# One triangular inverse corrected once a level and turned for its other form, a recurrence split by directions, and grouped attention heads written by channels

## The chip, the cores and the metric

One core of a Trainium2 chip runs the whole program in one launch. The metric is the device time of that core in microseconds (us). The kernel before took 3077.0 us, the median of three runs (3072.32 to 3078.3).

## The reference, cut to what matters

Two transformer blocks in float32, 512 latent and 256 context tokens, width 1024. The first block mixes tokens with two recurrences (a gated one, HG, and a gated delta rule, DN), then applies a mixture of experts. The second block has attention (four differential heads, eight grouped-query heads of 64 channels sharing two key/value heads), a gated MLP, a spatial gating unit and a second MLP. The adaptive modulation vectors of both blocks are products of a silu vector with a 1024 x 6144 matrix each (three matrices, 24 MB each).

The delta rule needs, for every chunk, direction and head, the solution of a unit lower triangular system, and then a scan over chunks:

```
a_mat = strict_lower(beta * k k^T * decay) + I
u, w  = solve(a_mat, [beta * v, beta * exp(cum) * k])
v_new = u_c - w_c @ state
o     = q_dec @ state + qk @ v_new
state = g_tot * state + k_dec^T @ v_new
```

This kernel takes chunks of 128 tokens (6 of them, `NC`), 4 heads in two passes of 2 (`p` = 0 and 1) and 2 directions, so that a chunk has four 128 x 128 systems. The grouped heads of attention are

```
s = q k^T * 64**-0.5 ; p = softmax(s) ; o = p v      (4 query heads share one k, v)
```

## The kernel before, in words

Each engine has its own instruction stream, and semaphores order them. The program is a list of stages (norm, hg0, hg1, dn0, dn1, wout, moe, proj, attn, awout, ffn0, sgu, ffn1) with a meeting of all engines after each. The change touches dn0 and dn1 (the delta rule's two passes), attn, and awout.

**The modulation chunks.** The product with the modulation matrices is cut into 72 chunks of 1 MB (`pe_mod_chunk`, L378, matmul at L385: four column tiles of 32 columns, each with 512 moving columns). SyncE loads them through a ring of slots, of which four serve these stages; the load of a slot is issued when TensorE has reported its last use. Eight chunks make a group; a group ends with a copy on ScalarE (L418), column sums on TensorE (L396) and a second copy on ScalarE (L424). `pe_mods(pe, W, count, end)` runs `count` chunks at a place of the TensorE program, and `act_mods` runs ScalarE's part at the place that answers to it. The lists at L995 say how many chunks stand where: `DN_MODS[p]` is (first, one per chunk of the system phase, one per unit of the inverse, a pair per step of the recurrence). Before, pass 0 has 8 at the start, none in system and inverse, 2+2+2+2 in the recurrence; pass 1 has 12 in the system phase, 8 in the inverse, 20 in the recurrence.

**Start of dn0** (`pe_dn_first`, L1036; `act_dn_first`, L1267). TensorE projects six tiles of pass 1 (L694, L686), runs 8 chunks (L385), turns the convolved q, k, v (L1048), projects two more tiles (L694) and turns the normed q, k (L1056). VectorE convolves (L1383) meanwhile; its last tap is followed by L1430. ScalarE, in order: the copies of the tiles, its part of the 8 chunks, silu of the convolved tiles (L1273, L1274), then the rest.

**System phase** (6 chunks). TensorE multiplies k k^T (and k q^T) (L1110, L1112) and the decay sums (L1115); GpSimd makes the masks (L1318) and multiplies by beta and the triangle (L1357, L1360, `mask_beta`); ScalarE takes exponentials (L1243); VectorE multiplies (L1455, L1457). In pass 0 the last six tiles of projection stand between the chunks.

**Inverse** (`products` L1138, `corrections` L1148). It is built level by level (7 levels, blocks of 1, 2, ... 64) and kept in two forms, XI and its transpose XT. A unit `u` is one chunk at one level, 42 per pass. GpSimd masks the level out of the system (`al`, L1334, two instructions). Level 0 is transposes (L1133) and subtractions. In each of the 30 units of levels 1 to 5 TensorE makes four products M = al^T XI (L1145), ScalarE copies M (L1252), TensorE makes eight corrections, four for each form (L1155, L1156), and VectorE subtracts them (L1473, L1474). The six units of the last level correct one form only. VectorE also runs two steps of the next pass's convolution per unit in pass 0 (L1383 and its neighbours).

**Recurrence** (6 steps). A step is KS = K dS (L1175), z on VectorE (L1488), U = X z (L1186), times beta on VectorE (L1497), ADD = kx^T dU (L1200), dS on VectorE (L1511). Each of these covers two directions and two heads: four matmuls, then one semaphore. Between KS and U and between U and ADD stand chunks (L385) or, in pass 0, groups of four transposes for pass 1 (`pe_tok_group`, L1077). `norm_steps` for pass 1 is handed out between VectorE's parts from step 3 on, and what is left runs after the last step. Then outputs (L1210, L1211), and in pass 0 more transposes (L1092).

**Attention** (`pe_attn`, L2454; 32 units, `u` from 16 on are grouped heads). TensorE runs scores(u+1) (L2462, eight records of 64 rows), values(u-1) and turn(u) (transposes of the probabilities, L2478). VectorE takes the maxima (L2534), ScalarE two exponentials of 128 x 768 (L2514), VectorE the reciprocals (L2557), and both copy the turned probabilities (L2523, L2525, L2554). scores(u+2) waits for both exponentials of unit u+1. For grouped heads turn(u) waits for the exponentials only; values is 12 matmuls with the turned probabilities as the weights and 64 value columns moving (L2494); VectorE divides by the sum on the way out (L2546). awout then turns all 1024 channels (eight transposes per 128 tokens, L1607), ScalarE copying four (L1648) and VectorE four (L1653), and multiplies by w_out (L1617).

A float32 matmul of 128 x 128 x 128 has two records on TensorE in this trace; a transpose has one.

## Time and profile before

| what | value |
|---|---|
| median of three runs | 3077.0 us |
| the profiled execution | 3088.53 us |
| its span, first to last instruction | 3086.6 us |
| mean granted TensorE clock | 0.956 |
| TensorE busy | 2854.6 us, 92% |
| VectorE, ScalarE, GpSimd busy | 1205.1, 579.2, 432.9 us |
| mean DMA rate | 131 GB/s |

Times below are microseconds from the start of the span. "x8" counts instruction records. A bracket at the end of a timeline row gives the idle time of that engine before the row, and what ended it. The granted clock is a share of full speed (2.4 GHz).

### The profile page before, as it was taken

What the parts mean: (1) busy time and instruction counts of PE and PEld (TensorE: products, weight loads), DVE (VectorE), ACT (ScalarE), POOL (GpSimd) and SP (SyncE); (2) the same over time, 40 slices, a digit from 0 to 9 for tenths busy, and PEclk for the clock granted to TensorE, in tenths of its full rate; (3) what the DMA queues carried; (4) which work ended last, traced back from release to release, by engine and by line L of the source; (5) the groups of instructions that cost most, each with busy time, mean ns of one, the idle gap of its engine ahead of it and who ended that gap; (6) DMA issues with size and microseconds to landing.
All of it is one profiled execution on the core that took longest, in us unless ns stands there. A gap on an engine that the chain in (4) does not pass through costs nothing.

```text
span 3086.6 us, 36191 instructions
## 1 busy us (share of the span) xinstructions
PE 2854.6 (92%) x14765; PEld 2144.3 (69%) x14765; DVE 1205.1 (39%) x2187; ACT 579.2 (19%) x1109; POOL 432.9 (14%) x507
## 2 busy tenths in 40 slices
PE   6999978987978599999999989899999999999998
PEld 4677646975944378788878758578874486688843
DVE  2173642873425211111132485366750102576601
ACT  2102012121201211111132255122110111211200
POOL 2152403525411100000000000000110000000100
PEclk8999978998989699999999999899999999999999
DMA  9211340024271599899982200032222221322220
GB/s 368 75 41 42 110 176 27 3 110 164 83 286 43 192 339 333 322 333 331 323 286 83 69 1 1 1 98 93 82 76 75 92 68 41 99 86 82 89 75 27
DMA packets 202849, 403.15 MB, mean 131 GB/s; under 512 B 12850, under 2 KB 100450, under 8 KB 193506
## 3 DMA queue, kind: packets, MB, share of 16 engines
...
q8 instruction: 91, 1.49, 0.2%
...
## 4 chain that ended last, share of the span: by engine, by line
PE 84%; DVE 6%; DMA 3%; ACT 3%; issue 2%; POOL 1%; ACTq 0%; SPq 0%; POOLq 0%; DVEq 0%
PE ps L2704 17%; PE ps L1891 11%; PE ps L694 7%; PE ps L1909 5%; PE ps L1617 5%; PE ps L2718 5%; PE ps L2320 4%; PE ps L2733 4%; PE ps L2891 4%; PE ps L686 3%; PE ps L764 2%; PE ps L2462 2%; PE ps L385 2%; PE ps L2494 2%; DMA ring<-in_w_mod 2%
## 5 line engine op out<-in xcount | busy, mean ns | idle before, releaser
L1891 PEld LDWEIGHTS ps<-arena,ring 128*128 128x128 f32 x2944 | 334.2, 193 | 13.3 <-issue 10.5
L1891 PE MATMUL ps<-arena,ring 128*128 128x128 f32 x2944 | 334.5, 276 | 2.4 <-DMA ring<-in_w_gate 2.4
L2704 PE MATMUL ps<-arena 128*128 128x256 f32 x1056 | 235.3, 379 | 1.6 <-DVE arena L2801 1.6
L2704 PEld LDWEIGHTS ps<-arena 128*128 128x128 f32 x1056 | 200.5, 190 | 29.6 <-DVE arena L2801 2.4
L1617 PE MATMUL ps<-ring,hT 128*128 128x512 f32 x384 | 172.7, 606 | 4.2 <-DVE arena L2947 2.6
L694 PE MATMUL ps<-hT,ring 128*128 128x512 f32 x384 | 171.5, 601 | 2.5 <-ACT bet L1034 1.8
L2704 PE MATMUL ps<-hT,ring 128*128 128x256 f32 x704 | 164.9, 389 | 3.3 <-ACTq L200 3.3
L1909 PE MATMUL ps<-ring,arena 128*128 128x512 f32 x368 | 164.0, 598 | 1.8
L2704 PEld LDWEIGHTS ps<-hT,ring 128*128 128x128 f32 x704 | 137.5, 196 | 23.8 <-ACTq L200 4.1
L2718 PE MATMUL ps<-ring,arena 128*128 128x512 f32 x352 | 151.5, 592 | 1.3 <-issue 1.3
L2733 PE MATMUL ps<-ring,arena 128*128 128x512 f32 x352 | 151.7, 592 | 0.0
L1334 POOL TENSOR_TENSOR arena<-arena,levm 128x256 f32<-128x256 f32 x168 | 124.4, 764 | 96.3 <-PE ps L1145 87.5
L1617 PEld LDWEIGHTS ps<-ring,hT 128*128 128x128 f32 x384 | 73.3, 195 | 91.3 <-issue 88.9
L2180 DVE TENSOR_TENSOR arena<-arena,ps 128x512 f32<-128x512 f32 x23 | 15.8, 688 | 303.7 <-PE ps L1891 303.7
L694 PEld LDWEIGHTS ps<-hT,ring 128*128 128x128 f32 x384 | 73.0, 193 | 87.0 <-issue 83.1
L2850 POOL TENSOR_TENSOR arena<-arena 128x512 f32<-128x512 f32 x44 | 56.6, 1286 | 509.9 <-DVE arena L2811 509.9
L2320 PE MATMUL ps<-ring,hT 128*128 128x256 f32 x576 | 125.2, 379 | 1.6 <-ACTq L200 1.6
L1909 PEld LDWEIGHTS ps<-ring,arena 128*128 128x128 f32 x368 | 68.0, 190 | 84.2 <-issue 84.2
L2718 PEld LDWEIGHTS ps<-ring,arena 128*128 128x128 f32 x352 | 66.7, 190 | 85.2 <-issue 85.2
L1712 POOL TENSOR_TENSOR xres<-xres,arena 128x512 f32<-128x512 f32 x24 | 31.7, 1321 | 664.9 <-DVE arena L1682 664.9
L2733 PEld LDWEIGHTS ps<-ring,arena 128*128 128x128 f32 x352 | 66.7, 190 | 83.2 <-issue 83.2
L2320 PEld LDWEIGHTS ps<-ring,hT 128*128 128x128 f32 x576 | 109.0, 190 | 16.5 <-ACTq L200 1.9
...
## 6 DMA issues: line engine op xcount, KB each, us to landing
...
```

The costliest lines, as they stand in the source:

```text
L385: last = pe.matmul(ps[32 * b:32 * b + 32, mod_bank(g), :], sil[:, k, :], w[:, 0, b * BANK:(b + 1) * BANK], start=(k == 0), stop=(k == KD - ...
L686: last = pe.matmul(ps[:, bank, 0:CW], hsrc[:, k, m * P:(m + 1) * P], w[:, k, :], start=(k == 0), stop=(k == KD - 1))
L694: last = pe.matmul(ps[:, bank, 0:n], w[:, k, j * P:(j + 1) * P], src[:, k, :], start=(k == 0), stop=(k == KD - 1))
L1334: last = g.tensor_tensor(al[u % 2][:, 2 * d:2 * d + 2, :], AT[:, c, 2 * d:2 * d + 2, :], bc(levm[:, l, d, :], [P, 2, P], 1), ALU.mult)
L1617: last = pe.matmul(ps[:, 2 * (m % 2) + half, :], hT[:, 4 * q + k, m * P:(m + 1) * P], ws[2 * half + q][:, k, :], start=(q == 0 and k == 0) ...
L1891: last = pe.matmul(ps[:, t, f * P:(f + 1) * P], w[:, k, f * P:(f + 1) * P], xg[:, 4 * c + k, :], start=(c == 0 and k == 0 and f == 0), sto ...
L1909: last = pe.matmul(ps[:, 2 + half, :], aT[:, 2 * c + k, :], w[:, k, half * 512:(half + 1) * 512], start=(c == 0 and k == 0), stop=(c == 1 ...
L2320: last = pe.matmul(ps[:, u % PB, 0:CW], hT[:, k, m * P:(m + 1) * P], w[:, k, :], start=(k == 0), stop=(k == KD - 1))
L2704: last = pe.matmul(ps[:, u % 8, 0:HTOK], a[:, k, :], b[:, k, :], start=(k == 0), stop=(k == KD // 2 - 1))
L2718: last = pe.matmul(ps[:, m, :], fa[:, q + k, m * P:(m + 1) * P], w[:, k, :], start=(q + k == 0), stop=(q + k == NF - 1))
L2733: last = pe.matmul(ps[:, 4 + m, :], fa[:, q + k, m * P:(m + 1) * P], ws[i][:, k, :], start=(q + k == 0), stop=(q + k == NF - 1))
L2891: last = pe.matmul(ps[:, u % 8, 0:CW], hT[:, k, m * P:(m + 1) * P], w[:, k, :], start=(k == 0), stop=(k == KD - 1))
```

## The change

In each unit of levels 1 to 5 only XT is corrected; the new `turned(u)` transposes the corrected XT on TensorE one unit later, and ScalarE copies it to XI, in place of four matmuls and VectorE's subtraction. The last level multiplies only 64 x 64 quadrants, placed by `tile_position`, and copies and subtracts only these. The recurrence's KS, U and ADD, their semaphores and their PSUM banks are one per direction. The chunks are placed anew: 4 before and 4 after the first transposes of pass 0, then 2, 14, 4 (system, inverse, recurrence); 6, 14, 8 in pass 1. Pass 1's last six tiles all use PSUM bank 7, each waiting for the copy of the one before, and the loads follow the new order (8 chunks, DNK, 2 chunks, DNV). The groups of transposes for pass 1 stand in steps 2 and 3, and the norm steps start at step 4. For grouped heads the probabilities are scaled before they are turned, one head by VectorE and one by GpSimd; values has 64 value columns as the weights in two column tiles and 128 probability columns moving, and writes channels by tokens, so that awout needs no transposes of them; the w_out rows of these heads are loaded in two parts to match. `fw_in`, `attn_in` and `sgu_in` are folded into `ctx_in` and `small_in`, with the counts changed to match.

```diff
             def take(self, a, width=SLOT, parts=1):
...
         def pe_units_between(pe, W, name, units, base, lo, hi):
             for u in range(lo, hi):
-                if u >= 2:
+                if name == "dnp" and base and u >= QZ + 2:
+                    pe.wait_ge(s[name + "_out"], base + u)
+                elif u >= 2:
                     pe.wait_ge(s[name + "_out"], base + u - 1)
-                pe_unit(pe, W, name, units, u, 6 + u % 2)
+                pe_unit(pe, W, name, units, u, dn_bank(base and 1, u) if name == "dnp" else 6 + u % 2)
...
-        DN_MODS = [KD, [0] * NC, [0] * NC * LEVELS, [(0, 2), (2, 0), (0, 0), (0, 0), (1, 1), (1, 1)]], \
-            [0, [2] * NC, [int(u in range(10, 42, 4)) for u in range(NC * LEVELS)], [(0, 0)] + [(2, 2)] * 5]
-        DN_TOK = [(0, 0), (0, 2), (2, 1), (1, 2), (0, 0), (0, 0)]
+        DN_FIRST = [4, 4]
+        DN_MODS = [[0, 2, 0, 0, 0, 0], [int(u in range(8, 36, 2)) for u in range(NC * LEVELS)], [(0, 0), (1, 0), (1, 0), (1, 0), (1, 0), (0, 0)]], \
+            [[1] * NC, [int(u in range(8, 36, 2)) for u in range(NC * LEVELS)], [(0, 0)] + [(1, 1)] * 3 + [(1, 0), (1, 0)]]
+        DN_TOK = [(0, 0), (0, 0), (2, 2), (2, 2), (0, 0), (0, 0)]
...
@@ pe_dn_first (act_dn_first has the same two places)
-            pe_mods(pe, W, DN_MODS[0][0], True)
+            pe_mods(pe, W, DN_FIRST[0], False)
             W.pay()
             pe.wait_ge(s["conv_done"], 1)
...
             last.then_inc(s["tok_ps"], 1)
+            pe_mods(pe, W, DN_FIRST[1], True)
             pe.wait_ge(s["mod_raw"], mods["pe"]["summed"])
...
@@ pe_dn, products(u)
-                pe.wait_ge(s["inv_out"], U0 + u - NC + 1)
+                if u < 2 * NC:
+                    pe.wait_ge(s["inv_out"], U0 + u - NC + 1)
+                else:
+                    pe.wait_ge(s["M_ready"], inv_ready(p, "x", u - NC))
...
                 for a in range(4):
-                    last = pe.matmul(ps[:, u % 2, a * P:(a + 1) * P], al[u % 2][:, a, :], XI[:, c, a, :], start=True, stop=True)
+                    if u < NC * (LEVELS - 1):
+                        last = pe.matmul(ps[:, u % 2, a * P:(a + 1) * P], al[u % 2][:, a, :], XI[:, c, a, :], start=True, stop=True)
+                    else:
+                        (lo, x), (hi, y) = sides(a // 2)
+                        last = pe.matmul(ps[hi, u % 2, a * P:(a + 1) * P][:, lo], al[u % 2][lo, a, hi], XI[lo, c, a, lo],
+                                         start=True, stop=True, tile_position=(x, y))
...
@@ pe_dn, corrections(u)
-                    if u // NC < LEVELS - 1:
-                        pe.matmul(ps[:, 2 + u % 2, a * P:(a + 1) * P], XT[:, c, a, :], m[:, a, :], start=True, stop=True)
-                    last = pe.matmul(ps[:, 4 + u % 2, a * P:(a + 1) * P], m[:, a, :], XT[:, c, a, :], start=True, stop=True)
+                    if u < NC * (LEVELS - 1):
+                        last = pe.matmul(ps[:, 4 + u % 2, a * P:(a + 1) * P], m[:, a, :], XT[:, c, a, :], start=True, stop=True)
+                    else:
+                        (lo, x), (hi, y) = sides(a // 2)
+                        last = pe.matmul(ps[lo, 4 + u % 2, a * P:(a + 1) * P][:, hi], m[hi, a, lo], XT[hi, c, a, hi],
+                                         start=True, stop=True, tile_position=(y, x))
                 last.then_inc(s["inv_ps"], 1)
+            def turned(u):
+                c = u % NC
+                pe.wait_ge(s["inv_out"], U0 + u + 1)
+                if u >= NC + 2:
+                    pe.wait_ge(s["M_ready"], inv_ready(p, "x", u - 2))
+                for a in range(4):
+                    last = pe.transpose(ps[:, 2 + u % 2, a * P:(a + 1) * P], XT[:, c, a, :], ident[:, :])
+                last.then_inc(s["M_ps"], 1)
             products(NC)
             for u in range(NC, NC * LEVELS):
                 if u + 1 < NC * LEVELS:
                     products(u + 1)
                 corrections(u)
-                pe_mods(pe, W, DN_MODS[p][2][u], False)
+                if NC <= u - 1 < NC * (LEVELS - 1):
+                    turned(u - 1)
+                pe_mods(pe, W, DN_MODS[p][1][u], u == NC * LEVELS - 1)
...
@@ pe_dn, the recurrence
             for k in range(NC):
                 if k:
-                    pe.wait_ge(s["dS_ready"], (NC - 1) * p + k)
                     for d in range(2):
+                        pe.wait_ge(s["dS_ready"], per_side(NC - 1, p, k - 1, d))
                         c = ORDER[d][k]
                         for h in range(2):
-                            a = 2 * d + h
-                            last = pe.matmul(ps[:, 0, a * P:(a + 1) * P], KT[:, c, h, :], dS[:, k - 1, a, :], start=True, stop=True)
-                    last.then_inc(s["ks_ps"], 1)
+                            last = pe.matmul(ps[:, KSB[d], h * P:(h + 1) * P], KT[:, c, h, :], dS[:, k - 1, 2 * d + h, :], start=True, stop=True)
+                        last.then_inc(s["ks_ps"], 1)
...
+        KSB, UB, AB = [0, 3], [1, 4], [2, 5]
+        def dn_bank(p, u):
+            return TURN_BANK if p and u >= QZ + 2 else 6 + u % 2
+        def per_side(steps, p, k, d):
+            return 2 * (steps * p + k) + d + 1
+        def sides(d):
+            first, second = (slice(0, 64), 0), (slice(64, P), 64)
+            return (first, second) if d == 0 else (second, first)
...
@@ act_dn, after the copy of M for unit u
+                if NC <= u - 2 < NC * (LEVELS - 1):
+                    a.wait_ge(s["M_ps"], inv_ps(p, "x", u - 2))
+                    a.activation(XI[:, (u - 2) % NC].rearrange("p a x -> p (a x)"), ps[:, 2 + u % 2, :], ACT.Copy).then_inc(s["M_ready"], 1)
...
@@ dve_dn, unit u of a level from 1 on
                     if l < LEVELS - 1:
-                        v.tensor_tensor(XI[:, c], XI[:, c], ps[:, 2 + u % 2, :].rearrange("p (a x) -> p a x", a=4), ALU.subtract)
-                    last = v.tensor_tensor(XT[:, c], XT[:, c], ps[:, 4 + u % 2, :].rearrange("p (a x) -> p a x", a=4), ALU.subtract)
+                        last = v.tensor_tensor(XT[:, c], XT[:, c], part, ALU.subtract)
+                    else:
+                        for d in range(2):
+                            (lo, _), (hi, _) = sides(d)
+                            x = XT[lo, c, 2 * d:2 * d + 2, hi]
+                            last = v.tensor_tensor(x, x, part[lo, 2 * d:2 * d + 2, hi], ALU.subtract)
...
-                    if p == 0 and k >= 3:
+                    if p == 0 and k >= 4:
                         next(norm, None)
...
@@ pool_dn
-            if p:
-                pool_mods(g, ch, 6)
+            pool_mods(g, ch, 7 if p else 4)
...
-            pool_mods(g, ch, MGROUPS if p else 4)
+            pool_mods(g, ch, MGROUPS if p else 5)
...
@@ pe_out and dve_turn_out
-                for k in range(KD):
+                for k in range(4 if j == 1 else KD):
...
+            if j == 1:
+                v.sem_inc(s["hT_dve"], 1)
+                return
...
@@ pe_attn, turn(u)
+                pe.wait_ge(s["probs_ready"], u + 1)
                 if g:
-                    pe.wait_ge(s["exp_done"], 2 * u + 2)
-                else:
-                    pe.wait_ge(s["probs_ready"], u + 1)
+                    pe.wait_ge(s["probs_pool"], u - ND + 1)
...
@@ pe_attn, values(u), the grouped heads
-                    for a in range(2):
-                        for j in range(NC):
-                            last = pe.matmul(ps[:, 7, a * HD:(a + 1) * HD], pt[:, 6 * a + j, :],
-                                             V[:, j, 512 + a * HD:512 + (a + 1) * HD], start=(j == 0), stop=(j == NC - 1))
+                    for j in range(NC):
+                        for a in range(2):
+                            last = pe.matmul(ps[HD * a:HD * (a + 1), 7, 0:P], V[:, j, 512 + a * HD:512 + (a + 1) * HD],
+                                             pt[:, 6 * a + j, :], start=(j == 0), stop=(j == NC - 1), tile_position=(0, HD * a))
...
@@ dve_attn
-                        for a in range(2):
-                            c0 = 512 + (h + 4 * a) * HD
-                            last = v.tensor_scalar(oat[:, m, c0:c0 + HD], ps[:, 7, a * HD:(a + 1) * HD], tw[:, 6 + a:7 + a], None, ALU.mult)
+                        last = v.tensor_copy(hT[:, 4 + h, m * P:(m + 1) * P], ps[:, 7, 0:P])
...
+                    else:
+                        pm = Pm[u % 2]
+                        v.sem_inc(s["sums_inverse"], 1)
+                        v.tensor_scalar(pm[:, 0, :], pm[:, 0, :], t[:, 6:7], None, ALU.mult).then_inc(s["probs_ready"], 1)
+        def pool_attn(g):
+            for u in range(ND, AU):
+                g.wait_ge(s["sums_inverse"], u - ND + 1)
+                x = Pm[u % 2][:, 1, :]
+                g.tensor_scalar(x, x, asm[:, u % 4, 7:8], None, ALU.mult).then_inc(s["probs_pool"], 1)
```

`inv_ps(p, what, u)` and `inv_ready(p, what, u)` are positions of a product ("m") or of a turned unit ("x") in the order in which TensorE and ScalarE run them. `z_ready`, `u_ps`, `u_ready`, `add_ps` and `dS_ready` are counted per direction in the same way as `ks_ps`.

## Rows read from the trace of the kernel before

**Rows 1.** The page, the chain that ended last, share of the span by engine

```profile
PE 84%; DVE 6%; DMA 3%; ACT 3%; issue 2%; POOL 1%; ACTq 0%; SPq 0%; POOLq 0%; DVEq 0%
```

**Rows 2.** Busy time by stretch, TensorE to GpSimd, then clock, DMA share, GB/s

```profile
432.50:492.70 60.20, 39.38 (x176) 22.83 (x174) 11.86 (x14) 16.00 (x26) 0.56 (x3) 0.70 0.42 157
550.00:646.90 96.90, 94.98 (x816) 94.31 (x817) 89.09 (x132) 24.28 (x39) 53.00 (x70) 0.97 0.01 2
646.90:687.90 41.00, 30.46 (x233) 21.08 (x233) 23.39 (x60) 9.19 (x13) 5.87 (x10) 1.00 0.43 157
702.70:736.10 33.40, 26.88 (x168) 13.50 (x168) 7.19 (x20) 5.66 (x9) 19.60 (x33) 0.90 0.77 294
751.10:855.60 104.50, 103.57 (x888) 95.53 (x888) 42.69 (x66) 22.02 (x38) 50.21 (x75) 0.99 0.21 72
855.60:922.90 67.30, 49.03 (x312) 26.60 (x312) 15.36 (x49) 2.24 (x6) 6.75 (x15) 0.84 0.79 300
1855.50:1923.00 67.50, 67.50 (x529) 55.89 (x528) 36.73 (x72) 35.51 (x72) 0.00 (x0) 1.00 0.00 1
```

**Rows 3.** Timeline of the start of dn0, single rows of three engines

```profile
432.47 0.21 DVE L1430 TENSOR_TENSOR dtmp<-dtmp,aldt 128x48 f32<-128x48 f32 x1
...
441.09 1.94 PE L385 MATMUL ps<-ring,gate 128*32 128x512 f32 x8 [3.60 <-DMA ring<-in_w_mod]
...
458.13 1.05 ACT L1273 ACTIVATE arena<-arena 128x1024 f32<-128x1024 f32 x1
...
472.83 7.03 PE L694 MATMUL ps<-hT,ring 128*128 128x512 f32 x16
485.54 4.50 PE L1056 MATMUL ps<-ident,arena 128*128 128x128 f32 x20 [5.69 <-DVE arena L1421]
```

**Rows 4.** Timeline of TensorE in the inverse; 30 such units a pass

```profile
550.03 3.78 PE L1145 MATMUL ps<-arena 128*128 128x128 f32 x16 [2.04 <-POOL arena L1334]
...
761.56 1.06 PE L1145 MATMUL ps<-arena 128*128 128x128 f32 x8
764.24 1.06 PE L1145 MATMUL ps<-arena 128*128 128x128 f32 x8
767.01 1.07 PE L385 MATMUL ps<-ring,gate 128*32 128x512 f32 x8
768.01 1.16 PE L1145 MATMUL ps<-arena 128*128 128x128 f32 x8
```

**Rows 5.** Timeline of TensorE, dn0's recurrence: four matmuls, then four transposes

```profile
659.77 1.16 PE L1175 MATMUL ps<-arena 128*128 128x128 f32 x8 [1.21 <-DVE arena L1511]
660.77 0.60 PE L1077 MATMUL ps<-ident,hT 128*128 128x128 f32 x4
```

**Rows 6.** Timeline of dn0's recurrence, starts of steps 4 and 5, and VectorE

```profile
674.39 1.16 PE L1175 MATMUL ps<-arena 128*128 128x128 f32 x8 [1.28 <-DVE arena L1511]
...
680.19 1.12 DVE L1511 SCALAR_TENSOR_TENSOR arena<-arena,dex,ps 128x128 f32<-128x128 f32 x4 [0.73 <-PE ps L1200]
...
681.37 1.16 PE L1175 MATMUL ps<-arena 128*128 128x128 f32 x8 [1.28 <-DVE arena L1511]
```

**Rows 7.** Timeline of GpSimd in dn1's system phase, and its end

```profile
718.62 1.18 POOL L1318 TENSOR_TENSOR arena<-cmask,lga 128x256 f32<-128x256 f32 x2 [0.54 <-PE ps L1115]
...
736.08 0.72 POOL L1334 TENSOR_TENSOR arena<-arena,levm 128x256 f32<-128x256 f32 x1
```

**Rows 8.** Timeline of TensorE in attention, differential heads, then grouped heads

```profile
1826.86 1.56 PE L2462 MATMUL ps<-arena 64*128 64x512 f32 x8 [0.84 <-ACT arena L2514]
...
1831.44 1.56 PE L2462 MATMUL ps<-arena 64*128 64x512 f32 x8 [0.84 <-ACT arena L2514]
...
1873.87 2.89 PE L2494 MATMUL ps<-arena 128*128 128x64 f32 x24
1876.60 1.48 PE L2478 MATMUL ps<-ident,arena 128*128 128x128 f32 x12
1878.01 1.56 PE L2462 MATMUL ps<-arena 64*128 64x512 f32 x8
```

201 lines of the change are left out of this document (122 added, 79 removed).

## The prediction

> **What bounds the kernel now.** Read the chain first: TensorE carries 84% of it, VectorE 6% [rows 1]. So time falls only where TensorE has less to do, or where a wait of TensorE is shortened. The table by stretch shows where it waits [rows 2]. In the two inverses (550 to 647, 751 to 856) it is busy 94.98 of 96.90 and 103.57 of 104.50 us. In the grouped heads it is busy all of 67.50 us, twelve units of 5.63. In dn0's recurrence it is busy 30.46 of 41.00, in dn1's system phase 26.88 of 33.40, in dn1's recurrence 49.03 of 67.30; the last two also show DMA shares of 0.77 and 0.79 near 300 GB/s and clocks of 0.90 and 0.84. There the chunks arrive too slowly: 12 and 20 of them are asked for in 33 and 67 us, about 3 us each, while in the inverses the DMA queues idle (0.01 and 0.21). At the start of dn0 VectorE is done with the convolution at 432.5, yet ScalarE's silu starts at 458.13 [rows 3]: in ScalarE's program it stands behind the eight chunks, one of which waits 3.60 us for its weights.
>
> **The change, part by part.** Negative is a gain. Unit prices: twelve matmuls take 764.24 - 761.56 = 2.68, so one is 0.223 and eight are 1.79; a chunk between units adds 768.01 - 764.24 - 2.68 = 1.09 [rows 4]. A switch from matmuls to transposes costs 660.77 - 659.77 - 0.89 = 0.11 [rows 5]; twelve transposes take 1878.01 - 1876.60 = 1.41, so four are 0.47 [rows 8].
>
> Start of dn0: with four chunks ahead, none of which ends a group, ScalarE's silu needs only the taps and runs at about 434.7 to 438.4. TensorE's fourth chunk ends at 441.09 + 1.94 = 443.0 [rows 3]; then it turns. The chunks five to eight follow at about 450.7 and their sums end near 459.5. DNK is now asked for after the fifth chunk is used, about 451.6, and I expect it by 459.5 as well. The two tiles, sqrt and norm then follow as before, and L1056 starts near 476.2 instead of 485.54: **-9.3**. Queued behind the late DNK are these two tiles and, on ScalarE, their copies and the square root.
>
> System phase of dn0: two chunks more, 2 x 1.09 = **+2.2**. The single bank makes each tile wait for the copy of the one before; between two tiles stand the matmuls of a system, about 1.9 us, more than a copy needs, so this is hidden. Without that cover it would be about 0.8 x 5.
>
> Inverse: a unit becomes 1.79 + 0.11 + 0.47 = 2.37 instead of 2.68, so 30 units take 71.1 instead of 80.4. VectorE, which in pass 0 was as full as TensorE (89.09 of 96.90), loses one of two subtractions and is not the next limit. turned(u-1) waits for VectorE's subtraction with products and corrections, 1.79, in between; products(u) uses a copy that is five units old. For the last level I take 1.5 a unit: below 1.79, which is what eight full matmuls cost, and above 1.2, GpSimd's two masks, taken from L1318's 1.18 for two of the same size [rows 7]. It could be as low as 0.9 for TensorE's part, and as high as 2.1 with the handovers. Pass 0: 14 chunks are new, 15.3, and two group sums, which I set at 2.5. -9.3 + 15.3 + 2.5 - 1.5 = **+7**. Pass 1: 8 chunks become 14, 6.5, one more sum, 1.3: -9.3 + 6.5 + 1.3 - 1.5 = **-3**.
>
> Recurrence: a step is 681.37 - 674.39 = 6.98 with two chunks in it and no wait for weights [rows 6]. It is three times four matmuls with their drain, 3 x 1.16, and three VectorE parts of 1.12, about 0.8 and 1.12, with handovers. By direction, each link is two matmuls and half of a VectorE part: 3 x (0.45 + 0.27) + 0.6 + 0.4 + 0.6 plus six handovers of about 0.08 = 4.2; the other direction runs in the gaps. A chunk between KS and U is half hidden (+0.4), one between U and ADD adds about 0.7. Pass 1: first step 2.5, three of 5.3, one of 4.6, last 4, sums 2: 29 instead of 67.3: **-38**. The bound from the other side is the old step: 5 x 7.0 + 7 = 42, a gain of 25. Eight chunks in 29 us is more than 3 us each, so the queue should keep up. Pass 0: 2.5 + 4.6 + 2 x 6.8 (four groups of transposes per step, each pair waiting once for a copy through one bank) + 5.8 + 5 = 31.5 instead of 41: **-9.5**. But the norm steps start one step later in a loop 10 us shorter: five of eleven are done in it instead of eight, and the first turned group of the output phase waits for the rest, about **+4**.
>
> System phase of dn1: six chunks less, no wait for weights. Next in line is GpSimd: its mask for chunk c+1 waits for TensorE, its triangles for VectorE; 19.60 us busy in 33.40 [rows 2], plus a start of about 5 until the first triangle. The inverse's first mask, at 736.08 before [rows 7], would come at about 728: **-8**.
>
> Grouped heads: TensorE's unit is scores 1.49, values 1876.60 - 1873.87 = 2.73, turns 1.41, together 5.63 [rows 8]. The values product has 24 records as before, now in two column tiles. A chunk's eight records of 512 columns in four column tiles take 1.07 [rows 4], while sixteen such records over the whole array take 7.03 [rows 3]: 0.13 against 0.44 each. So column tiles run side by side, and I take 1.4 for values, sum 4.3. Then the loop through the exponentials limits, which in the differential heads is 1831.44 - 1826.86 = 4.58, with TensorE idle 0.84 [rows 8]. GpSimd's scaling of 768 columns, 1.8 by three times L1318's 0.59 [rows 7], starts after the reciprocal and runs beside scores and values (2.9), so it is hidden; if values took 0 it would show by 0.5. VectorE gets about 0.6 more and has 36.73 of 67.50 filled. I take 4.75 a unit: 16 x 0.88 = **-14**. From the other side: records without overlap keep 5.63, 0.
>
> The Trainium skill, TensorEngine Tiling (Array Packing), Key Properties, says that changing the tiling mode drains the TensorE. That speaks against values in column tiles between scores in row tiles and turns over the whole array; no row isolates a drain. At 0.2 for each of two new switches a unit of 4.3 would be 4.7, and the sum 2 us worse.
>
> awout: four transposes less for each of four blocks, 4 x 0.47 = **-2**; VectorE's copies there lie beside matmuls, 0. One more wait count, two more load issues per w_out half long before they are needed, and the merged semaphores: 0; the cover is the ring, loaded a stage ahead, and if it failed it would be one landing, some 6 us.
>
> Sum: -9.3 + 2.2 + 7 - 3 - 38 - 9.5 + 4 - 8 - 14 - 2 = -70.6. The profiled execution took 3088.5 and would take 3018; the median of the runs is 11.5 less, so **3006**.
>
> **The rivals.** (a) Values gain nothing: weights of 64 columns and 24 loads set the pace, or the tiles don't overlap, so that the change doesn't do there what it says. For it: 64 moving columns before took as long per record as 128 columns do elsewhere (2.73 / 24 = 0.114 against 0.112), so something besides columns holds the pace. Against: the chunks' 0.13. 3006 + 14 = 3020. (b) The recurrence still waits for chunks or keeps steps of 7: for it, the DMA share of 0.79; against, two thirds fewer chunks. 3006 + 13 = 3019. (c) The chain subtraction, transpose, copy holds TensorE in each of 60 units; for it, VectorE's two convolution steps in pass 0 stand ahead of the next subtraction; against, 2.9 us of other TensorE work before the copy is needed. At 0.8 a unit 3006 + 48 = 3054. (d) Slower: the clock falls in the inverse because a quarter of its time is transposes. At the low level four products take 3.78 / 2 = 1.89 instead of 0.89 [rows 4], so a unit of 2.37 becomes about 4.7; over 60 units +140, 3146. It decides as soon as more than half of the units run low (70 / 2.33 = 30). Against it: in the grouped heads, 1.41 of 5.63 is transposes and the clock is 1.00 [rows 2, 8]. The Trainium skill, TensorE: Matmul & The Clock Gate, part 4, says that transpose mode does not count as TensorE being busy in the same way; by that rule (d) would come, and these rows do not agree.
>
> **How the numbers follow.** Forecast 0.62, (a) 0.18, (b) 0.09, (c) 0.07, (d) 0.04. The forecast's own range is 2985 to 3025: the bounds of the recurrence, of the last level and of the start. (a) and (b) lie inside it; reaching 3038 takes in both together and a part of (c), and leaves out about 1 in 10. Faster by over 0.2% (6 us, about what a measurement of this kernel can tell from no change) in all cases but (d) and an unnamed mishap: 0.95; same 0.01; slower 0.04.
>
> **What would show it.** L1273's successor starts before 440. TensorE's units in the inverse are 2.37 apart, 3.46 with a chunk. Steps of dn1's recurrence are 5.3, with no wait for in_ada_w. dn1's system phase ends with GpSimd as the releaser. Grouped units are 4.6 to 4.9 apart, with TensorE waiting for ScalarE. Wrong would be: a clock under 0.9 in the inverse, a wait of turned units for VectorE of over 0.3 each, or grouped units at 5.6.

## The result and the profile after

The changed kernel takes 2998.1 us, the median of four runs (2997.33 to 3005.45), against 3076.45 for the kernel before in four runs on the same chip: a ratio of 0.9752, 95% interval 0.9734 to 0.9771. The forecast of 3006 was 8 us too high, and the forecast's own range (2985 to 3025) held the time. The span of the profiled execution fell from 3086.6 to 2996.2 us, by 90.4.

The page of the changed kernel: busy times, and the chain that ended last.

```profile
PE 2777.2 (93%) x14509; PEld 2062.6 (69%) x14509; DVE 1164.6 (39%) x2137; ACT 613.4 (20%) x1181; POOL 477.2 (16%) x523
PE 69%; issue 20%; DVE 4%; ACT 3%; DMA 2%; POOL 1%; ACTq 0%; SPq 0%; POOLq 0%; DVEq 0%
```

TensorE has 77 us less to do, VectorE 40 less, ScalarE and GpSimd 34 and 44 more. The share of waits for DMA in the chain went from 3% to 2%, VectorE's from 6% to 4%. TensorE's 69% against 84% before [rows 1], and the 20% of "issue", are no effect of the change: for the changed kernel the view puts the stretch of the experts, 978 to 1514 us, down as one piece of "issue". Its code is as before, and TensorE is busy 524 of its 536 us.

The stages of the changed kernel, in the columns of [rows 2]; in order: dn0's inverse, recurrence and output, dn1's system phase, inverse and recurrence, thirteen grouped units of attention, and what follows its last scores.

```profile
532.65:632.53 99.88, 94.21 (x825) 78.53 (x825) 63.90 (x108) 39.63 (x75) 58.20 (x78) 0.94 0.40 138
632.53:667.37 34.84, 27.67 (x193) 21.18 (x194) 20.72 (x55) 11.25 (x13) 5.24 (x11) 0.95 0.36 121
667.37:685.52 18.15, 11.88 (x84) 11.03 (x85) 10.97 (x24) 3.21 (x6) 0.00 (x0) 0.91 0.18 59
685.52:712.25 26.73, 20.50 (x121) 11.24 (x121) 7.19 (x20) 5.66 (x9) 20.98 (x35) 0.91 0.62 215
725.72:822.35 96.63, 94.16 (x824) 78.54 (x825) 24.03 (x42) 39.62 (x75) 51.35 (x78) 0.96 0.42 143
822.35:852.17 29.82, 28.63 (x201) 19.92 (x202) 16.08 (x50) 0.86 (x3) 5.26 (x11) 0.92 0.71 250
1775.82:1842.80 66.98, 57.89 (x573) 42.51 (x572) 43.87 (x78) 38.49 (x78) 33.84 (x13) 1.00 0.01 1
1842.80:1856.33 13.53, 9.09 (x105) 7.14 (x105) 6.03 (x12) 5.13 (x10) 5.21 (x2) 1.00 0.00 1
```

The boundaries of the two traces, subtracted stage by stage:

| stage | before | after | change | forecast |
|---|---|---|---|---|
| start of dn0, gate sums to L1056 / L1073 | 85.3 | 74.1 | -11.2 | -9.3 |
| system phase, dn0 | 51.6 | 53.7 | +2.1 | +2.2 |
| inverse, dn0 | 96.9 | 99.9 | +3.0 | +7 |
| recurrence, dn0 | 41.0 | 34.8 | -6.1 | -9.5 |
| output, dn0 | 14.85 | 18.15 | +3.3 | +4 |
| system phase, dn1 | 34.9 | 26.7 | -8.2 | -8 |
| inverse, dn1 | 104.5 | 96.6 | -7.9 | -3 |
| recurrence, dn1 | 67.3 | 29.8 | -37.5 | -38 |
| output, dn1 | 11.95 | 9.45 | -2.5 | 0 |
| attention to its end | 180.2 | 167.1 | -13.1 | -14 |
| awout and everything behind | 1143.2 | 1139.9 | -3.3 | -2 |

Level 0 of the two inverses (12.9 and 13.5 us) is left out; it did not change. With 0.7 less between dn1 and attention these make -82.1. The other 8.3 of the 90.4 lie ahead of the stages that the change is about: the clock in the first 50 us was 0.84 in the profiled execution of before and 0.97 in this one. The same shows among the experiments, whose code is equal there: the stage's first sums start at 388 to 390 us in eight profiled executions and at 396 in four. It belongs to an execution, not to a kernel, so spans are compared below by stage. The medians fell by 78.3 only, since the profiled execution of before was 12 us slower than the median; 3 to 4 us of the -82.1 are of that kind too, most likely in the rows of dn1's output and of attention's end, which ran at a lower clock there.

Single rows of TensorE and its releasers in the changed kernel: the start of dn0, the first transposes of dn1's inverse, the starts of two steps of dn1's recurrence. A bracket is idle time and what ended it.

```profile
425.80 1.05 ACT L1357 ACTIVATE arena<-arena 128x1024 f32<-128x1024 f32 x1
432.01 1.93 PE L395 MATMUL ps<-ring,gate 128*32 128x512 f32 x8 [3.28 <-DMA ring<-in_w_mod]
434.08 4.59 PE L1064 MATMUL ps<-ident,arena 128*128 128x128 f32 x24
448.22 5.24 PE L704 MATMUL ps<-hcT,ring 128*128 128x256 f32 x16 [1.85 <-DMA ring<-in_w_in]
...
712.25 1.09 PE L1151 MATMUL ps<-ident,arena 128*128 128x128 f32 x4 [4.35 <-POOL arena L1419]
...
831.87 1.23 PE L1215 MATMUL ps<-arena,hT 128*128 128x128 f32 x8 [0.25 <-DVE arena L1599]
...
837.52 1.23 PE L1215 MATMUL ps<-arena,hT 128*128 128x128 f32 x8 [0.25 <-DVE arena L1599]
```

Silu (L1357) ran as soon as the taps were done, at 425.8, where it had stood behind the chunks until 458 [rows 3] (of the 32 us between these times 8 are the earlier start of the stage); the transposes follow the fourth chunk, which is held by its own weights for 3.28. dn1's first inverse transposes wait for GpSimd, as forecast. A step of dn1's recurrence with two chunks takes 837.52 - 831.87 = 5.65, has no wait for weights, and TensorE waits once, 0.25.

### The profile page after: what moved, and what is told of

Read it like the earlier page. It is cut to its first block, busy times and chain, and to the rows that moved or that the text cites. A ratio compares the mean times of both kernels' runs of the same rounds, so it can differ in the third digit from the quotient of the medians.

```text
span 2996.2 us, 35814 instructions
## 1 busy us (share of the span) xinstructions
PE 2777.2 (93%) x14509; PEld 2062.6 (69%) x14509; DVE 1164.6 (39%) x2137; ACT 613.4 (20%) x1181; POOL 477.2 (16%) x523
## 3 DMA queue, kind: packets, MB, share of 16 engines
q8 instruction: 89, 1.46, 0.2%
## 4 chain that ended last, share of the span: by engine, by line
PE 69%; issue 20%; DVE 4%; ACT 3%; DMA 2%; POOL 1%; ACTq 0%; SPq 0%; POOLq 0%; DVEq 0%
PE ps L2812 18%; PE ps L704 7%; PE ps L1704 5%; PE ps L2826 5%; PE ps L2420 4%; PE ps L2999 4%; PE ps L2841 4%; PE ps L696 3%; PE ps L1167 2%; PE ps L395 2%; PE ps L1181 2%; PE ps L776 2%; PE ps L2562 2%; DMA ring<-in_w_mod 1%; ACT arena L2613 1%
## 5 line engine op out<-in xcount | busy, mean ns | idle before, releaser
L1991 PEld LDWEIGHTS ps<-arena,ring 128*128 128x128 f32 x2944 | 334.2, 193 | 13.4 <-issue 10.5
L2420 PE MATMUL ps<-ring,hT 128*128 128x256 f32 x576 | 125.3, 379 | 1.6 <-ACTq L210 1.6
L2999 PE MATMUL ps<-ring,hT 128*128 128x256 f32 x512 | 113.5, 386 | 1.6 <-ACTq L210 1.6
```

The costliest lines, as they stand in the source:

```text
L1991: last = pe.matmul(ps[:, t, f * P:(f + 1) * P], w[:, k, f * P:(f + 1) * P], xg[:, 4 * c + k, :], start=(c == 0 and k == 0 and f == 0), sto ...
L2420: last = pe.matmul(ps[:, u % PB, 0:CW], hT[:, k, m * P:(m + 1) * P], w[:, k, :], start=(k == 0), stop=(k == KD - 1))
L2999: last = pe.matmul(ps[:, u % 8, 0:CW], hT[:, k, m * P:(m + 1) * P], w[:, k, :], start=(k == 0), stop=(k == KD - 1))
```

## The experiments

The recurrence, the start and the inverse came first, then attention, then two versions made from what was found. Numbers in "measured" are the median and the ratio to the kernel before, run on the same chip; 0.9752 (0.9734 to 0.9771) is the changed kernel's. The groups of experiments ran on different chips, so medians of two groups are compared only roughly.

### All eight chunks ahead of the first transposes

```diff
-        DN_FIRST = [4, 4]
+        DN_FIRST = [8, 0]
```

> The changed kernel with all eight chunks of the first group ahead of the first transposes, as before; all else new. My theory (ScalarE's silu stands behind the eight chunks' copy and holds the transposes): the silu starts again after 455 instead of near 430, the stretch from the last tap to the second transposes goes from 74.1 back to about 85, and the time is 2998 + 11 = 3009. Rival (the 11.2 us came from the new order of the loads, not from the split): the stretch stays within 3 us of 74 and the time at 2998 to 3001.

Measured: 3007.8 us, ratio 0.9786 (0.9754 to 0.9817). The timeline of ScalarE and TensorE in this kernel:

```profile
445.97 0.60 ACT L428 ACTIVATE gate<-ps 128x512 f32<-128x512 f32 x1 [18.91 <-PE ps L395]
446.46 1.05 ACT L1357 ACTIVATE arena<-arena 128x1024 f32<-128x1024 f32 x1
...
450.22 5.38 PE L1064 MATMUL ps<-ident,arena 128*128 128x128 f32 x24 [4.32 <-ACT arena L1358]
```

ScalarE idles 18.91 us for the end of the chunk group (L428), with its silu queued behind. The stretch to the second transposes grows by 9.8 us, which is the whole difference. The split of the group carries the start's gain, 9.8 of 11.2. The order of the loads is the changed kernel's here, so the rival falls. The silu began at 446.5, earlier than I had written: this execution was 7 us ahead of that of before when the stage began.

### The chunks where they stood before

```diff
-        DN_FIRST = [4, 4]
+        DN_FIRST = [8, 0]
-        DN_MODS = [[0, 2, 0, 0, 0, 0], [int(u in range(8, 36, 2)) ...], [(0, 0), (1, 0), (1, 0), (1, 0), (1, 0), (0, 0)]], \
-            [[1] * NC, [int(u in range(8, 36, 2)) ...], [(0, 0)] + [(1, 1)] * 3 + [(1, 0), (1, 0)]]
+        DN_MODS = [[0] * NC, [0] * NC * LEVELS, [(0, 2), (2, 0), (0, 0), (0, 0), (1, 1), (1, 1)]], \
+            [[2] * NC, [int(u in range(10, 42, 4)) ...], [(0, 0)] + [(2, 2)] * 5]
```

The places where group sums and GpSimd's `pool_mods` stand go back with them.

> The changed kernel with the chunks where they stood before (8, then 0, 0, 8 in pass 0; 12, 8, 20 in pass 1), and the new recurrence by directions, the new inverse and the new attention kept. Theory (dn1's recurrence was bound by the delivery of chunks, at about 3 us each, so that the placement and not the split by directions carries most of its 37.5 us): dn1's recurrence takes 60 to 67 us, its system phase 33 to 35, and the sum over all stages is 2998 + 11 (start) - 2 (system) - 17 (inverse of pass 0) + 3 (recurrence of pass 0) + 8 (system of pass 1) - 8 (its inverse) + 33 = 3026. Rival (the split by directions carries it): dn1's recurrence takes at most 45 and the time is about 3008.

Measured: 3024.7 us, ratio 0.9838 (0.98 to 0.9877). dn1's recurrence by stretch, and its waits for weights (in total, times, longest):

```profile
820.24:881.34 61.10, 43.72 (x312) 23.34 (x313) 16.25 (x50) 2.25 (x6) 6.77 (x15) 0.94 0.88 325
```

```profile
PE ps L395 <- DMA ring<-in_ada_w: 15.5, 12, 3.9
```

61.1 us with steps split by directions: 20 chunks of 1 MB in 61 us at 325 GB/s are 3.05 us each, the pace of the queue. Of the 37.5 us by which the stage shrank, the split alone gives about 6 and the placement the rest. The other stages moved too: both inverses are 16.3 and 10.5 shorter, having fewer chunks, dn0's recurrence 5.1 longer, dn1's system phase 12.2 longer (at 39.0 it is 4 longer than before the change and than I expected; the cause is open), the start 9.6 longer. Over all stages the placement is worth 26 us (3024.7 against 2998.1).

### Waits of the recurrence for both directions

```diff
         def per_side(steps, p, k, d):
-            return 2 * (steps * p + k) + d + 1
+            return 2 * (steps * p + k) + 2
```

> The changed kernel in which every wait of the recurrence is for both directions, so that a step is again three links of four matmuls with nothing of one direction beside the other; chunks stay where the change puts them. Theory: without chunk waits the old step of 7.0 us returns in dn1 (5.65 now), so dn1's recurrence is 29.8 + 5 x 1.4 = 37 and dn0's 34.8 + 4 = 39, the time 2998 + 11 = 3009, and the chunks' placement is worth the other 30 us of dn1's 37.5. Rival (the split is worth nothing, the steps are bound by the chunks between their links): both recurrences within 2 us and the time 2998 to 3001.

Measured: 3014.5 us, ratio 0.981 (0.9779 to 0.984). dn1's recurrence, then the starts of two steps:

```profile
829.20:870.18 40.98, 32.68 (x202) 21.63 (x202) 15.41 (x50) 0.98 (x3) 5.26 (x11) 0.82 0.51 183
```

```profile
844.02 1.16 PE L1215 MATMUL ps<-arena,hT 128*128 128x128 f32 x8 [1.21 <-DVE arena L1599]
...
850.85 1.16 PE L1215 MATMUL ps<-arena,hT 128*128 128x128 f32 x8 [1.22 <-DVE arena L1599]
```

A step is 6.83 instead of 5.65, as expected. The stage grew by 11.2. By steps: the first takes 5.82 for 3.59, at a granted clock of 0.50 in both kernels; the second 9.00 for 5.93, at 0.71 for 0.92; the next two 6.83 and 6.84 for 5.65 and the fifth 6.76 for 4.79, at full clock or nearly so; the last 5.73 for 4.21, at 0.72 for 1.00. So 4.3 us are steps at full clock, 2.2 the first step at half clock, and 4.6 come with a lower clock than the changed kernel had. dn0's recurrence grew by 9.6, again at a lower clock, 0.85 against 0.95. The other stages were 5.7 us shorter in small pieces. So with the chunks in their new places the split is worth 11 and 10, more than its steps at full clock show; with chunks in the old places it was worth 6 in dn1. The two parts help each other: a shorter step pays more when the weights are there.

### Both forms corrected by matmuls

```diff
@@ corrections(u), levels 1 to 5; turned(u) and ScalarE's copy go
+                        pe.matmul(ps[:, 2 + u % 2, a * P:(a + 1) * P], XT[:, c, a, :], m[:, a, :], start=True, stop=True)
@@ dve_dn
+                        v.tensor_tensor(XI[:, c], XI[:, c], ps[:, 2 + u % 2, :].rearrange("p (a x) -> p a x", a=4), ALU.subtract)
```

> The changed kernel with both forms corrected by matmuls and subtracted by VectorE again in levels 1 to 5 (eight corrections a unit, no transposes, no copy on ScalarE); last level and chunks stay new. Theory (a unit costs what TensorE has to do): 60 units of 2.68 instead of about 2.3, 60 x 0.38 = +23, time 3021, in pass 0 perhaps 5 more, where VectorE was 89.09 us busy of 96.90 before the change and now has 14 chunks less to hide behind than it needs. Rival (the handover subtraction, transpose, copy holds TensorE and the turning is worth less than 0.1 a unit): time 2998 to 3004.

Measured: 3027.3 us, ratio 0.984 (0.9811 to 0.9868). Both inverses of this kernel by stretch:

```profile
541.51:656.62 115.11, 107.90 (x945) 93.08 (x945) 94.25 (x138) 22.18 (x45) 61.95 (x78) 0.94 0.36 120
748.85:859.35 110.50, 107.58 (x945) 92.88 (x945) 41.90 (x72) 22.18 (x45) 51.21 (x78) 0.96 0.37 125
```

15.2 and 13.9 more than in the changed kernel: 0.49 for each of 60 units. In the changed kernel two units, the second with a chunk (L395), begin and end like this; L1195 is the four transposes:

```profile
600.61 1.16 PE L1167 MATMUL ps<-arena 128*128 128x128 f32 x8
...
602.50 0.60 PE L1195 MATMUL ps<-ident,arena 128*128 128x128 f32 x4
602.93 1.06 PE L1167 MATMUL ps<-arena 128*128 128x128 f32 x8
...
605.25 1.06 PE L395 MATMUL ps<-ring,gate 128*32 128x512 f32 x8
606.24 0.94 PE L1167 MATMUL ps<-arena 128*128 128x128 f32 x6
```

602.93 - 600.61 = 2.32, and 3.31 with a chunk. But the unit of 2.32 stands behind a chunk, and such a unit is 0.10 longer in every version: its first row is 1.16 where others have 1.06. Where no chunk is near, as in dn0's inverse with the chunks in their old places (the experiment above), a unit of the new form takes 2.22, 563.50 - 561.28:

```profile
561.28 1.06 PE L1167 MATMUL ps<-arena 128*128 128x128 f32 x8
563.50 1.06 PE L1167 MATMUL ps<-arena 128*128 128x128 f32 x8
```

That is to be held against 2.68 [rows 4], also a unit without a chunk. With chunks in every second unit the pairs are 3.31 + 2.33 in the changed kernel and 3.77 + 2.78 in the undone version, and the latter are the times of the units with a chunk, and behind one, in dn1's inverse before the change. So the gain is 0.46 a unit, 27 us of the 29 over both inverses, and a chunk costs 1.19: 1.09 where it stands and 0.10 in the unit behind it. TensorE has no wait between 545 and 617.

### The last level in whole blocks

```diff
@@ products, corrections, act_dn (if u < ...), dve_dn (if l < ...)
-                    if u < NC * (LEVELS - 1):
+                    if True:
```

> The changed kernel with the last level of the inverse in whole 128 x 128 matmuls, copies and subtractions again; all else new. Theory (the last level's six units take 15.0 us, of which TensorE's quadrants are little: the handovers from GpSimd's masks through ScalarE and VectorE set it, and whole blocks add what the copies and subtractions are longer, about 0.3 a unit, and TensorE's 1.79 of work): each pass gains at most 1 to 3 us from the quadrants, so the time is 2998 + 4 = 3002. Rival (the last level goes by TensorE's work: 1.79 against 0.3 a unit): 2 x 6 x 1.5 = 18 more, 3016.

Measured: 2995.7 us, ratio 0.9739 (0.9724 to 0.9753): no difference from the changed kernel. The two inverses:

```profile
541.58:640.48 98.90, 98.61 (x825) 84.07 (x825) 63.25 (x102) 39.84 (x69) 57.14 (x76) 0.98 0.41 139
732.39:831.45 99.06, 98.77 (x825) 84.23 (x825) 24.76 (x36) 39.83 (x69) 50.51 (x76) 0.98 0.42 139
```

dn0's inverse is 1.0 shorter with whole blocks and dn1's 2.4 longer, and the two recurrences behind them are 1.1 and 1.4 shorter. With quadrants TensorE has idle time, and what fills the last level is these rows of the changed kernel (dn0):

```profile
624.75 0.46 PE L1170 MATMUL ps<-arena 64*64 64x64 f32 x8 [1.00 <-POOL arena L1419]
...
625.82 1.68 DVE L1467 SCALAR_TENSOR_TENSOR hT<-ring,cols,hT 128x441 f32<-128x441 f32 x2
628.25 0.70 PE L1184 MATMUL ps<-arena 64*64 64x64 f32 x8 [1.07 <-DVE arena L1563]
```

GpSimd's masks and, in pass 0, VectorE, which puts two steps of convolution between two subtractions, set the pace. In dn0 the six units of the last level, without the column sums behind them, take 10.5 us with quadrants (620.3 to 630.8) and 10.3 with whole blocks; in dn1, where VectorE has no convolution, 6.5 and 10.3. So the quadrants gain nothing in dn0 and 3.8 us in dn1. Part of that is lost behind them: the column sums take 1.7 instead of 0.95, at half clock, and the first step of dn1's recurrence 3.59 instead of 2.55, at a clock of 0.50 instead of 1.00. The granted clock is 0.80 from 615 to 632.5 and 0.77 in the first 9.7 us of dn1's recurrence; with whole blocks it is 0.98 over both inverses. That quadrants must cost clock is not shown: in the first of the two versions at the end dn1's inverse and recurrence have the same code as here, run at 1.00 from 726 to 855, and take 94.5 and 28.3 instead of 96.6 and 29.8.

### Grouped heads and awout as before

The parts of the diff on attention and awout are taken back, word for word; the delta rule stays new.

> The changed kernel with the grouped heads and the output product of attention as before (scaling by VectorE on the way out, 64 value columns moving, eight transposes per 128 tokens in awout); the delta rule stays new. Theory (values in column tiles and the missing transposes are worth what the two traces show): units of 5.63 again, 16 x 0.47 = 7.5 more, 2 to 5 more in awout, time 2998 + 11 = 3009. Rival (most of the 18 us by which attention and awout shrank between the two traces was the clock, which is 0.9 or less there in some executions of any kernel): units of 5.63 but the time at most 2998 + 8 = 3006.

Measured: 3012.0 us, ratio 0.9792 (0.9769 to 0.9815). Thirteen grouped units and what follows:

```profile
1775.99:1849.16 73.17, 73.17 (x572) 60.57 (x572) 39.59 (x78) 38.30 (x78) 0.00 (x0) 1.00 0.00 1
1849.16:1867.53 18.37, 15.41 (x105) 13.94 (x105) 5.47 (x13) 5.13 (x10) 0.00 (x0) 0.83 0.00 1
```

Units of 5.63 against 5.16 (6.2 us over thirteen), 4.8 in the end of attention, and 2.4 behind it (1142.3 against 1139.9). The rival that called it the clock is right for a part of the 4.8 only: 0.83 there against 1.00.

### Both scalings on VectorE; GpSimd's in another form; VectorE's copy later

Between two grouped units of the changed kernel (VectorE, GpSimd and TensorE):

```profile
1796.49 0.69 DVE L2651 COPY arena<-ps 128x512 f32<-128x512 f32 x1 [1.64 <-PE ps L2577]
1797.10 0.15 DVE L2654 RECIPROCAL bet<-bet 128x2 f32<-128x2 f32 x1
1797.40 0.62 DVE L2664 TENSOR_SCALAR arena<-arena,bet 128x768 f32<-128x768 f32 x1
1797.41 2.60 POOL L2671 TENSOR_SCALAR arena<-arena,bet 128x768 f32<-128x768 f32 x1 [2.56 <-DVEq L2663]
1800.11 1.50 PE L2577 MATMUL ps<-ident,arena 128*128 128x128 f32 x12 [0.70 <-issue]
1801.65 0.69 DVE L2651 COPY arena<-ps 128x512 f32<-128x512 f32 x1 [1.64 <-PE ps L2577]
```

GpSimd's scaling ends at 1800.01 and TensorE turns at 1800.11. VectorE's copy of what is turned stands ahead of the next reciprocal in its program, and GpSimd waits for that: a ring of 5.16. TensorE's idle 0.70 is labelled "issue", but by the program it waits there for GpSimd's semaphore, and the times fit. Three kernels open the ring in different places.

```diff
@@ both on VectorE (GpSimd's and its wait go)
+                        v.tensor_scalar(pm[:, 1, :], pm[:, 1, :], t[:, 7:8], None, ALU.mult).then_inc(s["probs_ready"], 1)
@@ GpSimd's as a product of two tensors
-                g.tensor_scalar(x, x, asm[:, u % 4, 7:8], None, ALU.mult).then_inc(s["probs_pool"], 1)
+                g.tensor_tensor(x, x, asm[:, u % 4, 7:8].broadcast_to([P, TOK]), ALU.mult).then_inc(s["probs_pool"], 1)
@@ dve_attn: the copy, for u from 16 to 31, behind the scaling (turned_half holds its old lines)
                         v.tensor_scalar(pm[:, 0, :], pm[:, 0, :], t[:, 6:7], None, ALU.mult).then_inc(s["probs_ready"], 1)
+                        turned_half()
```

> The changed kernel with both heads' scalings of a grouped unit on VectorE (two of 0.62 us), none on GpSimd. Theory (a grouped unit takes 5.16 because GpSimd's scaling of 2.60 stands in a loop: reciprocal, scaling, turns, VectorE's copy, next reciprocal): the loop loses about 1.3 and the limit of the differential heads, 4.58, takes over: units of 4.6 to 4.7, 16 x 0.5 = 8 less, 2990. Rival 1 (switches of the tiling of TensorE set the unit): 5.16 stays, 2998. Rival 2 (VectorE fills up): units above 5.0.

> The changed kernel with GpSimd's scaling written as a product of two tensors, the second being the inverse sum broadcast along the row. Theory (GpSimd's product of two tensors takes 0.59 for 256 columns here, so 1.8 for 768, where its scaling by a column takes 2.60): the instruction takes about 1.8 and the unit falls from 5.16 to 4.6, 2990. Rival (GpSimd's price goes by the elements of this shape and not by the form): 2.5 or more and units of 5.1 or more, 2998.

> The changed kernel with VectorE's copy of the turned probabilities of unit u-1 placed behind the reciprocal and scaling of unit u in the grouped units, so that GpSimd's start no longer waits for that copy. Theory (the loop of 5.16 closes through the order of VectorE's program): GpSimd starts as soon as the exponentials are done, and units fall to 4.6 to 4.8, 2991. Rival (GpSimd's 2.60 holds the turns through the exponentials whatever VectorE's order): units of 5.0 or more, 2996 to 2999. Risk: the copy is late for values, which then wait up to 0.8.

Measured: 2991.8 us, ratio 0.9731 (0.9706 to 0.9755), units 4.66 and 4.69 in turn; 2995.0 us, 0.9733 (0.9712 to 0.9754), units 5.05 and 5.14 in turn; 2985.4 us, 0.9701 (0.9679 to 0.9722), units 4.59. Only the third is clear of the changed kernel by its time; the units of the first show its gain, 6.2 us over thirteen. The third reaches the limit of the differential heads, 4.58 [rows 8], with GpSimd's instruction still at 2.60:

```profile
1834.54 0.17 DVE L2656 RECIPROCAL bet<-bet 128x2 f32<-128x2 f32 x1 [0.94 <-ACT arena L2613]
1834.85 2.60 POOL L2674 TENSOR_SCALAR arena<-arena,bet 128x768 f32<-128x768 f32 x1 [1.99 <-DVEq L2665]
1836.17 1.53 PE L2593 MATMUL ps<-arena 128*64 128x128 f32 x24
1837.63 1.53 PE L2577 MATMUL ps<-ident,arena 128*128 128x128 f32 x12
1839.14 1.56 PE L2562 MATMUL ps<-arena 64*128 64x512 f32 x8
```

So VectorE's order closed the ring; taking GpSimd out of it opened it as well. In the second, GpSimd's instruction became faster than I had estimated, and almost nothing was won, 0.3 us over thirteen units:

```profile
1833.55 1.47 POOL L2671 TENSOR_TENSOR arena<-arena,bet 128x768 f32<-128x768 f32 x1 [3.58 <-DVEq L2663]
1833.56 1.87 DVE L2664 TENSOR_SCALAR arena<-arena,bet 128x768 f32<-128x768 f32 x1
```

VectorE's scaling, 0.62 beside GpSimd's other form, takes 1.87 here: it ends 0.4 after GpSimd's. It has in effect waited until GpSimd was done. VectorE's next maxima begin only at 1835.36, the exponentials wait for them and the scores for the exponentials, so the ring now goes through VectorE. The Trainium skill, SBUF — State Buffer, Who interferes with whom, says that the two engines share one pair of ports, taken for a whole instruction by whoever issues first, and that a VectorE scaling can be such a user; this pair of rows agrees.

### GpSimd's scaling without VectorE's beside it

```diff
                         v.sem_inc(s["sums_inverse"], 1)
-                        v.tensor_scalar(pm[:, 0, :], pm[:, 0, :], t[:, 6:7], None, ALU.mult).then_inc(s["probs_ready"], 1)
+                        v.sem_inc(s["probs_ready"], 1)
```

> The changed kernel without VectorE's scaling of the first head of the grouped units, which leaves that head's probabilities undivided by their sum; GpSimd scales the second head as before. Question: why GpSimd's scaling of 768 columns takes 2.60 where I estimated 1.8. Theory (it and VectorE's scaling of the same size, which start together, exclude each other, as VectorE's went from 0.62 to 1.87 beside GpSimd's product of two tensors; GpSimd then waits for VectorE's 0.62 first): alone GpSimd takes about 2.0, and units fall from 5.16 to about 4.6, time 2990. Rival (2.60 is what this form of instruction costs on GpSimd): 2.60 and 5.16 stay, time 2998.

Measured: 2994.0 us, ratio 0.9743 (0.9719 to 0.9767). GpSimd's sixteen scalings, in a view that groups instructions (count, busy us, mean ns of one):

```profile
L2671 POOL TENSOR_SCALAR arena<-arena,bet 128x768 f32<-128x768 f32 x16 | 35.3, 2206 | 284.5 <-DVEq L2663 284.5
```

2.21 alone, 2.60 beside VectorE's; units of 4.76. About 0.4 of the 2.60 comes with VectorE's scaling beside it, less than VectorE's whole 0.62, and 2.2 is what this form costs alone. Neither theory was quite right. The unit fell by 0.40, as much as GpSimd did, as a ring through GpSimd requires.

### Two versions from what was found

Both have VectorE's copy behind the scaling. The first spreads the groups of transposes over dn0's recurrence; the second does so too, and starts the norm steps at step 3 again.

```diff
-        DN_TOK = [(0, 0), (0, 0), (2, 2), (2, 2), (0, 0), (0, 0)]
+        DN_TOK = [(0, 0), (0, 1), (0, 2), (1, 1), (1, 1), (0, 1)]
@@ the second
+        DN_TOK = [(0, 0), (0, 2), (2, 1), (1, 1), (1, 0), (0, 0)]
@@ dve_dn, three places
-                    if p == 0 and k >= 4:
+                    if p == 0 and k >= 3:
```

> The changed kernel with VectorE's copy behind the scaling in the grouped units (as in the run before) and with the eight groups of transposes of pass 0's recurrence spread as 1, 2, 2, 2, 1 over steps 1 to 5 instead of four in step 2 and four in step 3. Theory (steps 2 and 3 take 8.0 us each because each pair of groups goes through one bank, so that its second group waits 0.69 for ScalarE's copy of the first, and steps with a chunk and no group take 4.9): single groups fall into gaps of the recurrence, steps 2 and 3 fall to about 6, the others grow by 0.5, dn0's recurrence goes from 34.8 to about 32, and with 8.5 from attention the time is 2987. Rival (each group costs its 1.3 wherever it stands): the recurrence stays at 34 to 35, 2990.

> As the run before it, with the norm steps of pass 1 again from step 3 on (before the change they were) and the groups as 2, 3, 2, 1 over steps 1 to 4. Theory (the norm's steps that are left behind the loop hold TensorE 3.1 us in the output phase of pass 0, where it took 14.85 before the change and takes 18.15 now): the output phase goes back to about 15.5, but three more norm steps of about 1.2 us stand in the loop, where VectorE is in the chain, so the recurrence grows by 2 to 3.5: together within 1.5 us of the run before it. Rival (the loop has room for them): 3 us less than it.

Measured: 2982.2 us, ratio 0.9705 (0.9689 to 0.9721), and 2981.0 us, 0.9697 (0.9682 to 0.9713). Recurrence and output of dn0, first version, then the second:

```profile
634.01:664.88 30.87, 26.48 (x193) 21.04 (x194) 20.76 (x55) 10.25 (x13) 5.24 (x11) 0.95 0.41 137
664.88:682.74 17.86, 11.60 (x85) 10.58 (x85) 10.97 (x24) 4.21 (x7) 0.00 (x0) 0.90 0.17 60
```

```profile
632.10:664.19 32.09, 26.96 (x194) 21.13 (x194) 22.00 (x59) 11.47 (x14) 5.24 (x11) 0.95 0.40 132
664.19:678.79 14.60, 10.25 (x84) 9.39 (x84) 9.45 (x20) 2.98 (x5) 0.00 (x0) 1.00 0.22 74
```

Spreading the groups takes 4.0 off the recurrence (34.8 to 30.9); the earlier norm steps, with the groups placed a little differently, cost 1.2 there and give back 3.3 in the output phase. Both are faster than the changed kernel (their intervals end below 0.9734), by 16 and 17 us of median. The stages that were changed, dn0's recurrence and output and attention, show 12.9 and 14.9 of it. The rest lies where the code is the same, in the first version above all in dn1's inverse and recurrence (2.2 and 1.5 less, at a higher clock). Between the two of them the times do not tell.

## Why the prediction was right, point by point

**Start of dn0: right.** Silu stood behind the group of chunks; the undone version returned 9.8 of 11.2 us. DNK arrived at 448.2. That is 3 us earlier than the 459.5 that I feared, not 11, since the stage began 8.3 us earlier than in the execution of before.

**System phases: right.** +2.1 in dn0, -8.2 in dn1, with GpSimd as the releaser of the first transposes (4.35 idle). Bank 7 for six tiles and the merged loads, taken at 0, were not tested by themselves.

**Inverse: mechanism right, sizes off; most of the 8 us by which the forecast was too high.** The mis-sized term is "1.79 + 0.11 + 0.47 = 2.37": the unit measured 2.22, since the four transposes take 0.43 in it with no switch on top. That is 13.7 us a pass instead of 9.3. A chunk was taken at 1.09 and costs 1.19, for the 0.10 in the unit behind it, which "a chunk between units" left out. By the two traces dn0's +3.0 is made of -13.7 for 30 units, +16.7 for 14 chunks, +3.0 for two column sums, -2.1 for the last level (12.6 to 10.5; forecast -1.5), -1.4 for the first unit, whose products ran at half clock before [rows 4], and +0.5 where the first quadrants hold the last whole unit. dn1's -7.9 is -13.7, +7.1 for six chunks, +1.7 for a sum, -4.3 for the last level (10.8 without its chunk to 6.5) and about +1.2 at the first and the last whole unit. So "1.5 a unit" for the last level was too low for dn0, 1.74, and too high for dn1, 1.08; GpSimd's masks and VectorE's convolution set the one, TensorE's and GpSimd's handovers the other.

**Recurrence of dn1: right for the stated reason,** 29.8 for 29. The nearness is in part luck: the first step takes 3.59 instead of 2.5, at half clock, and three steps 5.93, 5.65 and 5.65 instead of 5.3, while the last step and the sums take 4.2 instead of 6. And the prediction did not say how much each cause carries. The runs do: 67 before, 61 with the split alone, 41 with the placement alone, 30 with both.

**Recurrence of dn0: too optimistic by 3.4.** The step that failed is "2 x 6.8", for 2.4 of it; the first step, at half clock, is the rest, 3.45 instead of 2.5. Steps 2 and 3, with four groups each, took 8.0 (640.87, 648.87 and 656.86 are their starts), steps 1 and 4 took 4.9 and 5.6. A pair of groups waits 0.69 for the copy out of the one bank, in front of the chain both times; spreading them gave it back.

**Output of dn0: right,** +3.3; the remaining norm steps hold the first turned group for 3.08, and starting them a step earlier removed it.

**Grouped heads: the sum right by luck, its reason half wrong.** -13.1 for -14. Values went as taken (24 records in 1.46 instead of 2.73), so column tiles do run side by side and rival (a) is out. What failed is the step "GpSimd's scaling ... is hidden". It was priced from a product of two tensors at 0.59 per 256 columns, 1.8; it took 2.60, and the ring that it forms with VectorE's order was not seen. The unit became 5.16, not 4.75: 6.2 us less over thirteen units, where 4.75 would have given 11.4. The missing part came from the end of attention, which took 6.9 us less. It has three products with the values, which are shorter now, and it had run at a clock of 0.71 in the execution of before, against 1.00; I had counted only the first. Against the version with old heads, whose end ran at 0.83, this part of the change is worth 11.1 us in attention and 2.4 behind it.

**Switches of the tiling.** My reserve was 0.2 for each of two new switches, because the Trainium skill's page TensorEngine Tiling (Array Packing), Key Properties, says that a change of the mode drains TensorE. In the changed kernel the scores hold the values off by 1.50, against 1.49 before, so nothing shows at this one. The switch from values to turns is part of the 1.46 that values take, and no row separates it. Around a chunk, whose tiles are 32 columns wide, about 0.1 shows on each side: four transposes hold the next products off by 0.44 and a chunk by 0.53, and the products behind a chunk take 0.99 instead of 0.89.

**Rival (b)** fell for dn1 and held in part for dn0. **Rival (c)** fell: no wait of TensorE in the steady inverse. **Rival (d)** fell: the clock was 1.00 from 545 to 615 and from 735 to 810, with four transposes in each unit. I had read the Trainium skill (TensorE: Matmul & The Clock Gate, part 4), which says that a transpose does not count as TensorE being busy in the same way, to mean that these stretches would run low; they did not. But three quarters of each unit are matmuls. In level 0, where TensorE has nothing but transposes, the clock was 0.50 in dn1's pass, before and after alike, and 0.71 and 0.63 in dn0's; but TensorE is also idle for half of it (busy 6.66 of 13.5 us in dn1), so these rows do not tell the two causes apart. In the last level it fell to half at 625 and at 820, behind gaps of TensorE of 0.3 to 1.0 us.

**Not foreseen:** 2.5 us in the output of dn1 and a part of the 6.9 in the end of attention, both places that had run at a lower clock (0.78 and 0.71) and now ran at 1.00.
